# A fourth form of expert body, for 65 to 96 tokens, in a fused transformer step

## What is computed

```python
def moe_swiglu(h, w_router, b_router, w_in, w_out):
    logits = jnp.einsum('btd,de->bte', h, w_router, preferred_element_type=F32) + b_router.astype(F32)
    top_v, top_i = lax.top_k(logits, TOP_K)                # TOP_K = 2
    gates = jax.nn.softmax(top_v, axis=-1)
    dense_gate = jnp.sum(jax.nn.one_hot(top_i, N_EXPERTS, dtype=F32) * gates[..., None], axis=-2)
    out = jnp.zeros(h.shape, F32)
    for e in range(N_EXPERTS):                             # N_EXPERTS = 8
        out = out + dense_gate[..., e:e + 1] * swiglu(h, w_in[e], w_out[e]).astype(F32)
    return out.astype(h.dtype)
```

## Time and profile before

| | |
|---|---|
| median of 3 runs | 1946.71 us (1945.92 to 1959.38) |
| profiled execution | 1951.7 us, span 1950.2 us from the first to the last instruction |
| mean granted TensorE clock | 0.955 |
| PE busy | 1711.2 us, 88% |
| VectorE, ScalarE, POOL busy | 371.4, 316.5 and 100.8 us |
| moved by DMA | 529.73 MB, mean 272 GB/s |

### The profile page before, as it was taken

How to read it: one execution, slowest core, us unless ns; L and a number is a source line. 1 busy time by engine, 2 the same in 40 slices (tenths; PEclk the granted TensorE clock), 3 DMA queues, 4 the chain that set the end, 5 groups by cost and what they waited for, 6 DMA issues and landing times.

```text
span 1950.2 us, 29053 instructions
## 1 busy us (share of the span) xinstructions
PE 1711.2 (88%) x12350; PEld 1193.6 (61%) x12350; DVE 371.4 (19%) x1127; ACT 316.5 (16%) x942; POOL 100.8 (5%) x179
## 2 busy tenths in 40 slices
PE   5998989999999997978999877699998699997672
PEld 3556666767777745768975444299545399453431
DVE  2134333230000216541100101001001011010102
ACT  2223333220000124521000100000001000010102
POOL 1012110000000001001000000000000000000001
PEclk9999989999999997878999999999999899999996
DMA  9445878473434678344789999997769998899992
GB/s 347 169 141 197 283 286 279 166 259 130 138 104 125 242 190 272 108 164 148 287 319 320 396 392 388 402 374 274 265 226 391 397 386 311 313 387 403 383 403 99
DMA packets 259983, 529.73 MB, mean 272 GB/s; under 512 B 8297, under 2 KB 67353, under 8 KB 259714
## 3 DMA queue, kind: packets, MB, share of 16 engines
q1 hardware_dynamic: 248402, 496.67, 70.9%
q0 software_dynamic: 11440, 30.99, 4.9%
HBM read 506.13 MB, written 21.50 MB: 271 GB/s over the span
## 4 chain that ended last, share of the span: by engine, by line
PE 68%; DMA 16%; SPq 9%; DVE 2%; ACT 2%; issue 2%; POOL 0%; POOLq 0%; DVEq 0%
PE ps L1345 16%; PE ps L1220 9%; DMA big<-in_w_moe_in 8%; PE ps L1404 8%; PE ps L803 8%; DMA big<-in_w_moe_out 6%; PE ps L1327 6%; SPq L597 5%; PE ps L863 3%; DMA big<-in_w_ada 2%; PE ps L1241 2%; PE ps L769 2%; SPq L601 1%; PE ps L965 1%; PE ps L870 1%
## 5 line engine op out<-in xcount | busy, mean ns | idle before, releaser
L1345 PE MATMUL ps<-big 128*128 128x128 f32 (+1 forms) x2688 | 316.1, 282 | 22.5 <-DMA big<-in_w_moe_in 17.6
L1345 PEld LDWEIGHTS ps<-big 128*128 128x128 f32 x2688 | 315.6, 194 | 24.4 <-issue 24.4
L1327 PE MATMUL ps<-big 128*64 128x256 f32 x2240 | 258.7, 387 | 56.3 <-DMA big<-in_w_moe_in 51.6
L1327 PEld LDWEIGHTS ps<-big 128*64 128x64 f32 x2240 | 162.1, 139 | 146.9 <-DMA big<-in_w_moe_in 58.5
L1220 PE MATMUL ps<-work,big 128*128 128x288 f32 x704 | 172.8, 409 | 2.7 <-ACT work L1511 2.7
L1511 ACT ACTIVATE gqkv<-ps 128x144 f32<-128x144 f32 (+1 forms) x238 | 67.7, 311 | 616.9 <-PE ps L1345 309.1
L1384 PE MATMUL ps<-big,z 128*64 128x512 f32 x560 | 127.9, 598 | 42.2 <-DMA big<-in_w_moe_out 42.2
L1220 PEld LDWEIGHTS ps<-work,big 128*128 128x128 f32 x704 | 134.7, 192 | 40.3 <-issue 3.0
L2360 DVE TENSOR_TENSOR z<-ps,gqkv 128x256 f32<-128x256 f32 x224 | 68.9, 334 | 462.9 <-ACT gqkv L1511 462.9
L1404 PE MATMUL ps<-big,z 128*128 128x512 f32 x336 | 152.7, 602 | 2.2 <-DVE z L2360 2.2
L1384 PEld LDWEIGHTS ps<-big,z 128*64 128x64 f32 x560 | 38.1, 136 | 122.3 <-issue 69.4
(11 more groups left out here) (325 smaller groups left out, 1377.6 us busy)
## 6 DMA issues: line engine op xcount, KB each, us to landing
big<-in_w_moe_in SPq DMA_DIRECT2D x112, 2048.0 KB, 19.6
big<-in_w_moe_out SPq DMA_DIRECT2D x56, 2048.0 KB, 20.5
big<-in_w_ada SPq DMA_DIRECT2D x24, 2048.0 KB, 9.2
big<-in_w_ffd_in SPq DMA_DIRECT2D x22, 1024.0 KB, 7.7
big<-in_w_ffd_out SPq DMA_DIRECT2D x8, 1408.0 KB, 6.9
big<-in_cache_b_k SPq DMA_DIRECT2D x4, 2048.0 KB, 7.9
big<-in_cache_mla_ckv SPq DMA_DIRECT2D x64, 128.0 KB, 2.4
big<-in_cache_b_v SPq DMA_DIRECT2D x4, 2048.0 KB, 16.6
```

Source lines behind the costliest of these rows:

```text
L1327: last = mm(ps[64 * a:64 * a + 64, 512 * b + 256 * g:512 * b + 256 * g + 256], hsel[:, k, 0:NARROW], w[:, k, 256 * a:256 * a + 256], start ...
L1345: last = mm(bank(b, cols, 256 * g), w[g][:, k, 128 * i:128 * i + 128], hsel[:, k, 0:cols], start=(k == 0), stop=(k == KD - 1))
```

## The change

It adds a form *middle* for 65 to 96 tokens. The first 64 tokens go as in *small*. The other 32 (`hsel` columns 64 to 95) are a stationary operand of 32 columns on four column groups, each with its own quarter of the load's columns: 128 in the first product, 256 in the second. `act_turn` transposes a third block, VectorE copies it to the new `act_q`, and PE waits for one more group (`4*j+6`). The added columns use banks 1 and 7. *full* is left for 97 to 128 tokens. The branch at `over` now asks first for 96 tokens and then, in a new block `wide`, for 128. `rows_out` stores the rest in eight pieces instead of four in every form, with two more offsets, and `places` works these out.

```diff
-STORES = 7
+STORES = 11
+MIDDLE, QUARTER = 96, 32
@@ rows_out @@
-            def rows_out(row, row1, col1, row2):
+            def rows_out(row, row1, col1, row2, row3, row4):
...
                 for c in range(4):
-                    gp.dma_start(rows[bass.ds(row + P, EXTRA), 256 * c:256 * c + 256], o_rest[32 * c:32 * c + EXTRA, :]).then_inc(e_st, 16)
+                    gp.dma_start(rows[bass.ds(row3, 16), 256 * c:256 * c + 256], o_rest[32 * c:32 * c + 16, :]).then_inc(e_st, 16)
+                    gp.dma_start(rows[bass.ds(row4, 16), 256 * c:256 * c + 256], o_rest[32 * c + 16:32 * c + 32, :]).then_inc(e_st, 16)
@@ act_turn @@
-            def act_turn(it, j):
-
-                pe.wait_ge(e_act, NFE * it + (4 * j + 5))
+            def act_turn(it, j, cols):
+
+                pe.wait_ge(e_act, NFE * it + (4 * j + (6 if cols else 5)))
...
+                if cols:
+                    last = tp(bank(4, 128, 256), act_b[:, j, 0, 0:128], ident)
                 last.then_inc(e_t, 1)
@@ narrow_in @@
+                if cols:
+                    if j and g == 0:
+                        pe.wait_ge(e_act, NFE * it + (4 * j + 4))
+                    for k in range(KD):
+                        for c in range(4):
+                            last = mm(ps[32 * c:32 * c + QUARTER, 512 + 256 * g:512 + 256 * g + 128], hsel[:, k, NARROW:MIDDLE],
+                                      w[:, k, 128 * c:128 * c + 128], start=(k == 0), stop=(k == KD - 1))
@@ narrow_out @@
+                        for c in range(4 if cols else 0):
+                            last = mm(ps[32 * c:32 * c + QUARTER, 512 * 7:512 * 7 + 256], act_q[:, q, 32 * i:32 * i + QUARTER],
+                                      w[:, i, 256 * c:256 * c + 256], start=(q == 0 and i == 0), stop=(q == FCH - 1 and i == 3))
@@ first_pass @@
-                        pe.br_cond(tokens_of(e) > P, on_true=f"most{e}", on_false=f"full{e}")
+                        tokens = tokens_of(e)
+                        pe.br_cond(tokens <= MIDDLE, on_true=f"middle{e}", on_false=f"wide{e}")
+                    with nc.body(f"wide{e}", valid_engines=[pe.engine]):
+                        pe.br_cond(tokens > P, on_true=f"most{e}", on_false=f"full{e}")
                     large(e, P, f"full{e}", f"over{e + 1}")
                 for e in range(NE):
-                    large(e, CAP, f"most{e}", f"past{e}")
...
+                    for cols, name in ((MIDDLE, "middle"), (CAP, "most")):
+                        large(e, cols, f"{name}{e}", f"past_{name}{e}")
...
@@ places @@
-                link(V.tensor_scalar(row2, row2, float(TRASH), None, ALU.add))
...
+                V.tensor_scalar(row2, row2, float(TRASH), None, ALU.add)
+                V.scalar_tensor_tensor(out=row4, in0=base, scalar=float(80 - TRASH), in1=over, op0=ALU.add, op1=ALU.mult)
+                link(V.tensor_scalar(row3, row1, 64.0, None, ALU.add))
+                link(V.tensor_tensor(row4, base, row4, ALU.subtract))
+                link(V.tensor_scalar(row4, row4, 80.0, None, ALU.add))
@@ turned_copy @@
-                    V.tensor_copy(actT[:, j, :], bank(4, 256)).then_inc(e_tc, 1)
+                    V.tensor_copy(actT[:, j, :], bank(4, 256))
+                    V.tensor_copy(act_q[:, j, :], bank(4, P, 256)).then_inc(e_tc, 1)
```

## The result

Over ten runs each, the changed kernel takes 1937.55 us (median, 1930.5 to 1944.76) and the kernel before 1950.18 us (1945.92 to 1959.38). The ratio is 0.9933, with a 95% interval of [0.9914, 0.9952]: 13 us less, and less than 1%, which counts as no change by the bound of the prediction. The forecast was 1931 us in a range of 1923 to 1944. Of the 6.5 us by which the median lies above it, 3.5 are the kernel before, whose median was 1946.71 over three runs and 1950.18 over ten.

A forecast was written before the change was run, and what follows sets the result against it. Bound: the weight stream in narrow bodies, PE in expert 5's wide body. -19.9 + 1.5 + 2.0 + 0.8 + 0.3 + 0.15 = -15.2 us from the median 1946.71 gave 1931.5, so 1931 us; range 1923 to 1944.

The forecast's parts named there:

- The bound and the size of the prize: Expert 5's wide body: PE holds up the weight stream, which loses 19.9 us, the most there is to get.
- PE, 132.4 predicted: Expert 5's new body on PE: summed from rows of similar shapes to 132.4 us, against 152.8.
- The switch price: Expert 5's new body: 0.18 us for each switch of matmul form and back, 14 times in first product, 28 in second.
- The start: Ahead of expert 5's body: two gaps after jumps following expert 4's last matmuls, so PE starts at 1552 us.
- The margin: Early expert 6 loads: PE ends expert 5 at 1686.4 us, just early enough; 0 to 4 us lost, 1.5 taken.
- The stream's sum: Stream lost 19.9 us; given back: 1.5 late loads, 0.8 extra stores, 0.3 code fetches, 0.15 compares in experts 0 and 3.
- the wait for c6: Expert 6's seventh first-product load, issued only when expert 5's last load is consumed: 0 to 4 us lost, 1.5 taken.
- The tail: After the last expert: four more store issues on POOL at 496 ns lie on the path, +2.0 us.
- (a): Expert 5's body: PE slower than its rows, 4 to 15 us of gain lost, 1935 to 1946 us; chance 0.2.
- (b): Expert 5's body: instructions arrive too slowly, a 4.7 us gap with each of 13 packets, 1993 us; chance 0.06.
- (c): Stream stays full, costs smaller: one jump, no late-load loss, free stores; -17.9 us or more, 1924 to 1929; chance 0.22.
- (d): Expert 5: router places one more token, so it stays wide and the form is unused; 1949 us; chance 0.02.

The follow-up runs named there:

- no_quarter: Changed kernel with expert 5's new body run without its 32-token part (tokens 64 to 95 left out); 1940.20 us, ratio 0.9939 to the kernel before.
- pad7: Changed kernel with 7 idle matmuls of 512 columns added in the middle of expert 5; 1947.66 us, one execution.
- padded kernels: Changed kernel with 7 or 16 idle matmuls of 512 columns added in the middle of expert 5; 1947.66 and 1952.24 us, one execution each.
- fall_through: Changed kernel with expert 5's new body directly behind its branch, one jump instead of two; 1933.02 us, ratio 0.9923 to the kernel before.
- four_fall: Changed kernel with four stores of 32 rows and expert 5's body directly behind its branch; 1930.08 us, ratio 0.9900 to the kernel before.

## Why the prediction was right

**The bound and the size of the prize.** The step that carries the forecast is that expert 5 costs the stream 19.9 us and not PE's 152.8. The best stretch of any kernel is 348.3, so 19.1 us were there; at c13 of expert 6, where I had worked the number out, it is 215.7 - 196.5 = 19.2 with no_quarter. A reader who had taken PE's saving as the gain would have been at 24.0 and would not have seen that a body 48 us shorter than the old one (no_quarter, from 1555.67 to 1660.41) would bring hardly more than this one.

**PE, 132.4 predicted, 128.8 measured.** The rows from other stages carried over: 64 records of the four-group shape took 1.95 us, as in the earlier trace rows, and a load of the first product 5.49 (1557.91 to 1563.40) against 3.53 + 1.95. The switch price was too high. A slice of the second product takes 1.58 (1632.12 to 1633.70) against 0.92 + 0.56, so 0.10 for a switch and back, and in the first product 5.49 - 5.48 leaves 0.01, where I had 0.18 for each: 4.6 us too many in all (14 x 0.17 and 28 x 0.08). The Trainium skill (TensorEngine Tiling (Array Packing), Key Properties) has every change of tiling mode drain TensorE; the rows agree that the second product pays something, and show the price to lie near nothing where 64 records stand between two changes. In the other direction the first load went for the most part at the lower clock (granted 0.55 from 1549 to 1556, against 1.00 from 1556 to 1560; 0.50 is the 1.2 GHz level), after PE had stood for 11.14 us: 6.36 us instead of 3.60, 2.8 lost where I had 1.3 from the earlier trace rows. So the sum came closer than its terms.

**The start.** Two gaps at the price of the earlier trace rows put it 14.1 us behind q6 of expert 4, and it was 14.8 (1534.88 to 1549.67). The 2 us for a further gap inside the body did not occur here; pad7 shows that such a gap exists, 3.57 us, once.

**The margin.** My steps put PE's end 148.5 us behind that q6 (1686.4 - 1537.93) and called 1.5 of them lost, so the last free point at 147.0. The padded kernels put it at 147.0. To meet it that closely is luck, since the 1.5 was picked from 0 to 4. PE itself came in 4.9 us sooner than forecast, and so on the free side; c13 of expert 6 stood on PE 197.9 us behind q6 (1732.75 - 1534.88), where the forecast was 195.8 and 1.5 of loss. PE began to wait for loads again at 1716.51, three loads before c13, where I had expected c12 or c13.

**The stream's sum.** -19.9 + 1.5 + 0.8 + 0.3 + 0.15 made -17.15; measured is -17.4. The small terms can't be told apart at this size. The eight packets of code, against five forecast, all belong to the new body, since no_quarter has 111 again. The loss put at 1.5 is there in size: c13 of expert 6 comes 1.4 us later than in no_quarter. But it comes only 0.2 later than in fall_through, whose PE ends 6.6 us sooner, so most of it is not the wait for c6 that I had in mind. Between fall_through and no_quarter lie 0.11 MB of code, some 0.3 us by an estimate at 392 GB/s; the rest stays open.

**The tail is the term that was mis-sized: +2.0 forecast, +5.8 measured.** The issues were nearly right, 2.7 instead of 2.0: a store in this chain steps by 0.58 us and not by the 0.496 of the earlier trace rows, 2.3 for four, and another 0.35 is there with four stores too. The 0.55 in the gather is scatter. The 2.6 at the end of the program were missing from the sum, and nothing in the kernel before could give their price: it shows 10.0 us behind its chain, but not what they depend on. With the measured tail my sum would be -17.15 + 5.8 = -11.4 instead of -15.2. The measured ratio allows both (its interval is 9.4 to 16.8 us), so the time alone would not have shown this error; the stretches do.

**The rivals.** My case was 1929 to 1935, and the median of 1937.55 lies outside it, in the 1935 to 1946 of (a). But (a), PE slower than its rows, did not happen: PE was faster, 3.5 of the 6.5 us are the kernel before, and the longer tail covers the rest. As a difference, 12.6 us, it lies in my case. (b) Instructions too slow: no gap with issue inside expert 5, and in the seven profiles of this body one in all, the 3.57 us of pad7. (c) The stream keeps full, costs smaller, 1924 to 1929: two jumps were there, the stream gained 17.4 and not 19.9, and the tail took more than 2.0. four_fall, with one jump and the shorter tail, comes close, with 1930. (d) The form runs.

## What to carry to other kernels

When a stage alternates between a bound by a stream and a bound by an engine, size the gain by what the stream lost in the slow body, and find the point up to which the engine may be late: beyond it each microsecond counts, short of it hardly any. Rows of the same shape from other stages price a new body well, to 3% here, though errors of 4.6 us in the switches and 1.5 in the clock went in opposite directions. Count what a change adds to every iteration and to the end of the program, even where the iteration hides it: 32 more stores took back over a quarter of the gain (2.3 and 2.6 of 17.4 us), and packing the same rows into four stores instead of eight returned most of it.

## What the runs showed of the hardware that I had not expected

- The program's end grows with the transfers that POOL has issued in it: 10.0 us behind the last work in the three profiles with four stores for each expert, 12.6 in the seven with eight stores or as many transfers, 82 ns for each of the 32 more.
- Of two jumps of PE in a row to code that is not at hand, beside a full stream, leaving one out takes 6.2 us from the gap; the 4.92 us that then remain are like the 4.7 to 4.9 of the earlier trace rows.
- Alternating between two and four column groups costs at most 0.10 us for a switch and back.
